# First layer's experts: the rows of two experts gathered in one indirect DMA onto 128 partitions and turned by eight transposes

## The reference, cut to what matters

```python
D_MODEL = 1024; N_EXPERTS = 32; EXPERT_HIDDEN = 512
...
    def expert_block(args):
        xe, e = args
        return (jax.nn.silu(xe @ w_gate[e]) * (xe @ w_up[e])) @ w_down[e]

    y = lax.map(expert_block, (xb, blk_e)).reshape(cap, d)
    out = jax.ops.segment_sum(y.astype(jnp.float32) * w_buf[:, None], tok_buf, num_segments=t + 1)
```

## Time and profile before

| what | value |
|---|---|
| median of the runs | 2399.06 us (2398.18, 2399.06, 2402.39) |
| span of the profiled execution | 2400.5 us |
| PE busy | 2173.3 us, 91% |
| DVE busy | 1108.4 us, 46% |
| ACT busy | 692.3 us, 29% |
| POOL busy | 215.8 us, 9% |
| data moved | 656.73 MB, 274 GB/s mean |
| first layer's experts | about 1198 to 1716 us of the span |
| second layer's experts | about 1907 to 2375 us |

### The profile page before, as it was taken

How to read it: one execution, slowest core, us unless ns; L and a number is a source line. 1 busy time by engine, 2 the same in 40 slices (tenths; PEclk the granted TensorE clock), 3 DMA queues, 4 the chain that set the end, 5 groups by cost and what they waited for, 6 DMA issues and landing times. The chain is left out here.

```text
span 2400.5 us, 29499 instructions
## 1 busy us (share of the span) xinstructions
PE 2173.3 (91%) x11404; PEld 1361.6 (57%) x11404; DVE 1108.4 (46%) x1760; ACT 692.3 (29%) x1102; POOL 215.8 (9%) x330
## 2 busy tenths in 40 slices
PE   7999999998899999988898888888788899999996
PEld 5778788876777888856633333333366533333332
DVE  5677655465676456577511111111587522222223
ACT  4243344344334443366111110110237111111110
POOL 2000000010000001100111111111120000000000
PEclk9989999999999999999799999998889899999998
DMA  8745576573655657501799999999830799999995
GB/s 295 260 151 190 193 235 202 184 277 135 226 206 193 211 171 248 163 2 39 301 335 401 411 409 411 406 408 411 302 84 8 299 380 428 428 428 429 428 428 230
DMA packets 175600, 656.73 MB, mean 274 GB/s; under 512 B 16295, under 2 KB 61943, under 8 KB 150288
## 3 DMA queue, kind: packets, MB, share of 16 engines
q1 hardware_dynamic: 159648, 622.65, 67.6%
q0 software_dynamic: 14032, 30.00, 4.0%
q10 hardware_dynamic: 1824, 2.73, 0.3%
HBM read 649.97 MB, written 23.79 MB: 281 GB/s over the span
## 5 line engine op out<-in xcount | busy, mean ns | idle before, releaser
L750 PE MATMUL bank<-sb_ring_rounded,sb_hT_rounded 128*128 128x512 f32 x2432 | 605.7, 397 | 18.7 <-DVE sb_ring_rounded L2045 8.4
L1382 PE MATMUL bank<-sb_ring,sb_arena 128*64 128x512 f32 x1984 | 491.1, 640 | 94.1 <-DMA sb_ring<-in_w_up 91.3
L750 PEld LDWEIGHTS bank<-sb_ring_rounded,sb_hT_rounded 128*128 128x128 f32 x2432 | 459.4, 191 | 119.5 <-issue 12.9
L1382 PEld LDWEIGHTS bank<-sb_ring,sb_arena 128*64 128x64 f32 x1984 | 152.4, 146 | 378.7 <-issue 372.9
L2045 DVE TENSOR_TENSOR sb_ring_rounded<-sb_ring,sb_ring_rounded 128x2048 fp32r<-128x2048 f32 (+1 forms) x142 | 314.9, 2258 | 112.4 <-ACT sb_ring_rounded L1516 107.4
L750 PE MATMUL bank<-sb_ring_rounded,sb_arena_rounded 128*128 128x512 f32 x1408 | 356.8, 395 | 7.6 <-DVE sb_arena_rounded L2032 7.0
L1516 ACT ACTIVATE sb_ring_rounded<-sb_ring 128x2048 fp32r<-128x2048 f32 x146 | 268.1, 1887 | 125.7 <-PE bank L750 100.1
L750 PEld LDWEIGHTS bank<-sb_ring_rounded,sb_arena_rounded 128*128 128x128 f32 x1408 | 266.1, 190 | 63.3 <-DVE sb_arena_rounded L2032 7.3
L1926 ACT ACTIVATE sb_hb<-bank 64x512 f32<-64x512 f32 x64 | 37.8, 590 | 697.4 <-PE bank L1382 697.4
L1406 PE MATMUL bank<-sb_ring,sb_arena 128*64 128x512 f32 x1008 | 233.4, 606 | 3.5 <-DVE sb_arena L2877 3.5
L2877 DVE COPY sb_arena<-bank 128x256 f32<-128x256 f32 x64 | 27.1, 424 | 319.2 <-PE bank L1393 319.1
(11 more groups left out here) (372 smaller groups left out, 2121.9 us busy)
## 6 DMA issues: line engine op xcount, KB each, us to landing
sb_ring<-in_w_down SPq DMA_DIRECT2D x63, 2048.0 KB, 22.0
sb_ring<-in_w_up SPq DMA_DIRECT2D x62, 2048.0 KB, 21.3
sb_ring<-in_w_gate SPq DMA_DIRECT2D x62, 2048.0 KB, 16.9
sb_ring<-in_w_ada SPq DMA_DIRECT2D x48, 1024.0 KB, 7.5
sb_ring<-in_ffn_w_gu SPq DMA_DIRECT2D x44, 1024.0 KB, 7.8
sb_ring<-in_xa_w_kv SPq DMA_DIRECT2D x16, 1024.0 KB, 7.3
sb_ring<-in_ffn_w_down SPq DMA_DIRECT2D x16, 1024.0 KB, 6.4
sb_ring<-in_od_w_in SPq DMA_DIRECT2D x12, 1024.0 KB, 7.7
```

Of the source, the lines that this page charges most:

```text
L750: ins = pe.matmul(bank[b][0:rows, :], rnd(x), rnd(w[:, k, :]), start=start and k == k0 and q == 0, stop=stop and k == k1 - 1 and q == len( ...
L1382: ins = pe.matmul(bank[2 * j + part][part * ROWS:(part + 1) * ROWS, :], mxT[:, j, k, :], w[:, k, :], start=k == 0, stop=k == KD - 1)
```

## The change

`mx` becomes one tile of 128 partitions: the rows of the even expert of a pair lie on partitions 0 to 63, those of the odd one on 64 to 127. The token part of `idx` gets a second half: partitions 64 to 127 hold the tokens of the next expert, so one column lists the rows of two experts. This takes a second DVE instruction of the same size, and POOL waits for both. There is one gather for a pair, at the head of POOL's pair (j = 0) and always through a copy into `pick`, the first one too. PE turns both experts at once by eight 128 x 128 transposes in the place behind the matmuls of the odd expert (j = 1), into two banks; ACT copies them out in two halves behind the odd expert's `silu`. ACT zeroes half as much. SP waits for the one gather where it waited for the first of two. The second layer is computed as before.

```diff
-        idx = spare[0:ROWS, :].bitcast(U32).rearrange("p (a b) -> p a b", a=2)
+        idx = spare[:, :].bitcast(U32).rearrange("p (a b) -> p a b", a=2)
...
-        mx = view(0, 2, D)
+        mx = view(0, D)
...
-                    sp.wait_ge(m["rows0"], 16)
+                    sp.wait_ge(m["rows"], 16)
...
-                def turn_rows(j, e, landed_rows):
-                    pe.wait_ge(m[f"rows{j}"], landed_rows * 16)
+                def turn_gathered(i):
+                    pe.wait_ge(m["rows"], (i + 1) * 16)
                     pe.sem_inc(s["passed"], 1)
                     for k in range(KD):
-                        ins = pe.transpose(bank[T0 + j][:, k * ROWS:(k + 1) * ROWS], mx[0:ROWS, j, k:D:KD], ident[0:ROWS, 0:ROWS])
-                    ins.then_inc(m["pe_xT"], 1)
+                        ins = pe.transpose(bank[T0 + k // 4][:, k % 4 * P:(k % 4 + 1) * P], mx[:, k:D:KD], ident)
+                        if k % 4 == 3:
+                            ins.then_inc(m["pe_xT"], 1)
...
-                        pe.wait_ge(m["xT"], i * 4 + 4 if l else e + 1)
+                        pe.wait_ge(m["xT"], i * 4 + 4 if l else i * 2 + 2)
...
-                        if l == 0 and not (last and j == 1):
-                            turn_rows(1 - j, e + 1, i + 1 + j)
+                        if l == 0 and j == 1 and not last:
+                            turn_gathered(i + 1)
...
-                    zeros = cst[:, C_WIN0:C_WIN0 + P].unsqueeze(1).to_broadcast([P, 2 * KD, P])
-                    act.activation(view(0, 2 * KD, P), zeros, ACT.Copy).then_inc(s["rows_zeroed"], 1)
+                    zeros = cst[:, C_WIN0:C_WIN0 + P].unsqueeze(1).to_broadcast([P, KD, P])
+                    act.activation(view(0, KD, P), zeros, ACT.Copy).then_inc(s["rows_zeroed"], 1)
...
-                        if l == 0 and more:
-                            turned_rows(1 - j, e + 1)
+                        if l == 0 and j == 1 and not last:
+                            placed_turned(i + 1)
...
-                dve.tensor_scalar(idx[:, 1, :], idx[:, 0, :], 1, None, ALU.logical_shift_right).then_inc(*c.up(s["idx_ready"]))
+                for half in range(2 - l):
+                    n = BLK * N_EXP - half
+                    dve.tensor_scalar(idx[half * ROWS:(half + 1) * ROWS, 1, 0:n], idx[0:ROWS, 0, half:half + n], 1, None, ALU.logical_shift_right).then_inc(*c.up(s["idx_ready"]))
...
-            def gather(j, e):
-                since(pool, m["pe_xT"], e - 1)
+            def gather(i):
+                since(pool, m["pe_xT"], i * 2)
                 apart()
-                if isinstance(e, int):
-                    pool.sem_inc(m["picked_in"], 1)
-                    at = column(1, e)
-                else:
-                    pool.tensor_copy(pick[:, 0, j:j + 1], column(1, e)).then_inc(m["picked_in"], 1)
-                    pool.wait_ge(m["picked_in"], e + 1)
-                    apart()
-                    at = pick[:, 0, j:j + 1]
-                pool.indirect_dma_start(out=mx[0:ROWS, j, :], out_offset=None, in_=DR["tok"],
-                                        in_offset=bass.IndirectOffsetOnAxis(ap=at, axis=0),
-                                        bounds_check=tiles * P - 1, oob_is_err=False).then_inc(m[f"rows{j}"], 16)
+                pool.tensor_copy(pick[:, 0, 0:1], column(1, i * 2, P)).then_inc(m["picked_in"], 1)
+                pool.wait_ge(m["picked_in"], i + 1)
+                apart()
+                pool.indirect_dma_start(out=mx, out_offset=None, in_=DR["tok"],
+                                        in_offset=bass.IndirectOffsetOnAxis(ap=pick[:, 0, 0:1], axis=0),
+                                        bounds_check=tiles * P - 1, oob_is_err=False).then_inc(m["rows"], 16)
...
-                    if l == 0 and not last:
-                        gather(j, i * 2 + j + 2)
+                    if l == 0 and j == 0 and not last:
+                        gather(i + 1)
...
-                gather(0, 0)
-                gather(1, 1)
+                gather(0)
```

More of the change, by code:

```diff
@@ L164, in build_program @@
         mod_g, mod_one = fix[0:96, 0, :], fix[0:96, 1, :]
-        pick = sb("pick", [ROWS, 2, 2], U32)
+        pick = sb("pick", [P, 2, 2], U32)
         steps_i = sb("steps_i", [P, 1], I32)
@@ L192, in loop_sems @@
         def loop_sems(l):
-            by_rows = ["places", "equals", "marked"] if l else ["rows0", "rows1", "picked_in"]
+            by_rows = ["places", "equals", "marked"] if l else ["rows", "picked_in"]
             names = ["landed%d" % q for q in range(SLOTS + 2 + l)] + by_rows + [
@@ L1445, in experts @@
                 if l == 0:
-                    turn_rows(0, 0, 1)
+                    turn_gathered(0)
                 expert_steps(pe, less_2, pair)
@@ L1889, in experts @@
                 m = moe[l]
-                def turned_rows(j, e):
-                    act.wait_ge(m["pe_xT"], e + 1)
-                    act.activation(mxT[:, j, :, :], bank[T0 + j][:, :].rearrange("p (k n) -> p k n", k=KD), ACT.Copy).then_inc(m["xT"], 1)
                 def rows_out(i):
@@ L1901, in placed_turned @@
                     for half in range(2):
-                        act.wait_ge(m["pe_xT"], i * 4 + half + 3)
+                        act.wait_ge(m["pe_xT"], i * 4 + half + 3 if l else i * 2 + half + 1)
                         act.activation(mxT[:, :, 4 * half:4 * half + 4, :], bank[T0 + half].rearrange("p (k j n) -> p j k n", k=4, j=2), ACT.Copy).then_inc(m["xT"], 1)
@@ L1921, in pair @@
                         e = i * 2 + j
-                        more = not (last and j == 1)
                         act.wait_ge(m["pe_hidden"], e + 1)
@@ L1953, in experts @@
                 if l == 0:
-                    turned_rows(0, 0)
+                    placed_turned(0)
                 expert_steps(act, less_2, pair)
@@ L3040, in experts, with column @@
                     pool.wait_ge(*c.next(s[f"tok_stored{q}"], 16 * tiles // 2))
-            pool.wait_ge(*c.next(s["idx_ready"]))
+            pool.wait_ge(*c.next(s["idx_ready"], 2 - l))
             def apart():
                 pool.sem_inc(s["passed"], 1)
-            def column(kind, e):
-                return idx[:, kind, e:e + 1] if isinstance(e, int) else idx[:, kind, bass.ds(e, 1)]
-            def gather(j, e):
-                since(pool, m["pe_xT"], e - 1)
+            def column(kind, e, rows=ROWS):
+                return idx[0:rows, kind, e:e + 1] if isinstance(e, int) else idx[0:rows, kind, bass.ds(e, 1)]
+            def gather(i):
+                since(pool, m["pe_xT"], i * 2)
                 apart()
-                if isinstance(e, int):
-                    pool.sem_inc(m["picked_in"], 1)
-                    at = column(1, e)
-                else:
-                    pool.tensor_copy(pick[:, 0, j:j + 1], column(1, e)).then_inc(m["picked_in"], 1)
-                    pool.wait_ge(m["picked_in"], e + 1)
-                    apart()
-                    at = pick[:, 0, j:j + 1]
-                pool.indirect_dma_start(out=mx[0:ROWS, j, :], out_offset=None, in_=DR["tok"],
-                                        in_offset=bass.IndirectOffsetOnAxis(ap=at, axis=0),
-                                        bounds_check=tiles * P - 1, oob_is_err=False).then_inc(m[f"rows{j}"], 16)
+                pool.tensor_copy(pick[:, 0, 0:1], column(1, i * 2, P)).then_inc(m["picked_in"], 1)
[4 more added lines that the diff above has]
+                                        bounds_check=tiles * P - 1, oob_is_err=False).then_inc(m["rows"], 16)
             def store(j, e):
-                pool.tensor_copy(pick[:, 1, j:j + 1], column(0, e)).then_inc(m["picked_out"], 1)
+                pool.tensor_copy(pick[0:ROWS, 1, j:j + 1], column(0, e)).then_inc(m["picked_out"], 1)
                 pool.wait_ge(m["picked_out"], e + 1)
@@ L3074, in store @@
                 apart()
-                pool.indirect_dma_start(out=DR["y"][l], out_offset=bass.IndirectOffsetOnAxis(ap=pick[:, 1, j:j + 1], axis=0),
+                pool.indirect_dma_start(out=DR["y"][l], out_offset=bass.IndirectOffsetOnAxis(ap=pick[0:ROWS, 1, j:j + 1], axis=0),
                                         in_=my[0:ROWS, j, :], in_offset=None,
```

2 lines of the change are left out of this document (1 added, 1 removed).

## The result

The changed kernel takes **2379.24 us** (median of 4 runs, 2377.72 to 2380.78); the kernel before, in the runs beside it, 2399.87 us (4 runs, 2398.18 to 2402.39). The ratio is 0.9913, 95% interval 0.9902 to 0.9925: 20.6 us less, where the forecast was no change (2399.6, range 2391.0 to 2404.5).

The account below looks back on a forecast made before the run. From 1280 us on the DMA weight stream was taken as the bound, so saved PE time becomes waiting. Terms +1.9 - 0.4 - 1.0 = +0.5 us on 2399.06 gave 2399.6 us, range 2391.0 to 2404.5.

Parts of the forecast that it names:

- Bytes of the gathers: Weight stream beside the first layer's gathers: bytes unchanged, loss of 21 us taken as unchanged, 0, between -21 and +21.
- The test named at the end: Forecast wrong if the middle's rate leaves 405 to 415 GB/s, gather windows change depth, or PE waits for rows or `xT`.
- The start: Second table instruction, copy, first 128-row gather and turning two experts before the first matmul: +1.9 us, between +0.3 and +4.2.
- Holes filled: Up to 1280 us, expert 1's matmuls follow at once and SP issues earlier, filling weight-stream holes: -0.4 us, at most -0.65.
- Later turnings: Eight transposes for sixteen in each later pair: PE gets about 1.0 us a pair, the up-weight wait grows, 0.
- POOL's order: Gather in POOL's queue behind the store at a pair's head lands after perhaps 13 us, needed 22 us later: 0.
- End of the stage: Last pair: expert 31's turning goes, PE is the bound and everything behind moves up, -1.0 us; 0 if something else holds.
- The faster one: Gathers spread over all partitions stop holding up the weights: half the loss gone 2389.1 us, all 2378.6; chance 0.13.
- The slower one: Twice the rows in flight hold up the weights more, 28 us instead of 21: +7, 2406.6 us; chance 0.08.
- The expensive start: Copy waits and 128 rows take POOL twice as long: +4.2 at the start, 2402.3 us or 2403.3; chance 0.09.

Follow-up runs that it names:

- the dropped rows: Both kernels with every token index out of bounds, gathers issued but all rows dropped: 2369.32 us for the kernel before, 2368.01 us for the changed one.
- narrow-transpose run: The changed kernel with sixteen 64-row transposes per pair, into one bank for each expert, instead of eight wide ones: 2383.13 us.
- the two 64-row gathers: The changed kernel with its 128-row gather issued as two of 64 rows, onto partitions 0 to 63 and 64 to 127: 2403.00 us.
- the padded one: The changed kernel with a second, nearly empty gather issued behind each gather: 2374.19 us, beside 2380.11 us for the changed kernel.
- the two with the 128-row form in the kernel before: The kernel before, 32 gathers issued over 128 partitions, half the rows dropped: 2390.92 us landing on partitions 0 to 63, 2380.39 us with halves in turn.
- doubled gathers: Each gather issued a second time: changed kernel, 128-row gathers onto an unread region, 2381.35 us; kernel before, 64-row gathers onto partitions 64 to 127, 2433.40 us.
- lower-half run: The kernel before with each gather issued over 128 partitions, upper half's indices out of bounds, rows still on partitions 0 to 63: 2390.92 us.

## Why the prediction was wrong

**The step that failed** is *Bytes of the gathers*: "I take the value of an unchanged number of rows, since few rows cost little and many cost much". The bound was right (21 us; the dropped rows price it at 20.9), the place was right (the gathers' windows), and the value inside the bounds was wrong: the same rows cost 20.9 us over their bytes in the 64-row form and 1.3 or less in the 128-row form. My reason for zero rested on two windows that differ in rows, and both were of 64 partitions, so they could say nothing on 128; between -21 and +21 the zero was a midpoint and not a reading. The test named at the end, a middle outside 405 to 415 GB/s, is what happened.

**The other steps.** *The start*, +1.9 forecast. From the end of the table's first instruction (1193.70, the middle of L2845's pair; 1197.15 before) to SP's load are 19.7 us for 17.74 before: +2.0. The sum was right and its terms were not, so this is luck. Table and copy cost 0.6 where 0.3 was forecast; from issue to the transposes there are 5.20 us for 5.85, so the 128 rows do not land 0.8 later but 0.65 earlier; turning costs 2.63 for 1.81, +0.8 as forecast; and expert 0's matmuls take 1.2 more up to SP's load (10.13 for 8.92), which the forecast did not have. The eight wide transposes need 1.95 us here, at a granted clock of 0.50, and not the 1.13 of the earlier trace rows, at 1.00: "the clock hardly matters" was wrong, and the +0.8 came out because the wait for ACT behind them is 0.69 us here for 1.44 there. The 1.2 us are the clock as well. These are the windows of 1209 to 1210 us, before and after, with the granted clock in the third column from the end:

```profile
1209.00:1210.00 1.00, 1.00 (x6) 0.28 (x4) 0.00 (x0) 0.00 (x0) 0.00 (x0) 0.69 0.88 377
```

```profile
1209.00:1210.00 1.00, 1.00 (x6) 0.31 (x4) 0.00 (x0) 0.00 (x0) 0.00 (x0) 0.82 0.30 107
```

By them the clock rose from 1.2 to 2.4 GHz at about 1209.6 and 1209.4 us, almost the same moment, but expert 0's matmuls had begun at 1205.97 and at 1203.28: 3.6 and 6.1 us of them ran at half speed, and half of the difference is 1.2 us.

*Holes filled*, -0.4, at most -0.65: too small. The first 65 us from SP's load on, in the kernel before and the changed one, then in both without rows:

```profile
1214.89:1279.89 65.00, 62.63 (x308) 24.75 (x308) 13.84 (x22) 10.08 (x17) 9.78 (x16) 1.00 0.99 379
```

```profile
1213.41:1278.41 65.00, 60.27 (x288) 22.53 (x286) 13.84 (x22) 9.75 (x17) 7.96 (x14) 0.99 0.99 404
```

```profile
1214.48:1279.48 65.00, 62.43 (x308) 24.66 (x309) 13.85 (x22) 10.09 (x17) 9.95 (x17) 1.00 0.97 384
```

```profile
1212.24:1277.24 65.00, 61.65 (x292) 22.98 (x290) 13.85 (x22) 9.75 (x17) 8.99 (x15) 0.98 0.98 401
```

Without rows the changed kernel still moves 401 GB/s for 384, which is worth 65 x 17/428 = 2.6 us of the stream, an estimate. No gather's form can do that; expert 1 follows without a gap (46 matmuls in one group), and SP issues the next weights sooner (7.6 us behind the first load, for 9.6). A share of 0.99 did not bound the holes at 0.65 us, since the share does not show the rate. In the middle, where the gathers' form acts, 375 x (426 - 409)/428 are 15 us of the stream, so that some 15 to 17 of the 19.6 us are the form's. Why the gain of the beginning does not show in the equal stretches of the two kernels without rows stays open; it is of the size of their scatter.

*Later turnings*, 0: right within the scatter, by the narrow-transpose run. But the wait for the up weights grew by 3.5 us and not 10 (69.9, 22 times, for 66.4, 25 times). That the weights, which came sooner too, took up the rest is argued and not shown.

*POOL's order*, 0: right. A gather lands after 11.7 us in the median and 14.2 at most (13 forecast), and PE waits for rows only once, at the start.

*End of the stage*, -1.0: nothing. The turning is gone from behind 1656.94, but the last up weights come at 1664.23, and PE waits 3.68 us for them: the time saved lies in a wait. "PE is the bound there" was true of the kernel before, where these matmuls begin at 1686.63 without a wait, and is not of the changed one.

**The rivals.** The faster one had the place and the size right, and as its mechanism the destination spread over all partitions, which the two 64-row gathers refute. The slower one expected deeper gather windows; they vanished. The expensive start came to half of its upper bound.

## What to carry to other kernels

Where a stream of weights over 128 partitions saturates the DMA engines, give every small load beside it the same 128-partition form, even if half of its rows are dropped, and then fill both halves evenly: here 1024 rows cost 30.7 us in the 64-row form and 11.0 or less in the other. Look for the loss in GB/s at a full share, not in the share: 410 and 426 GB/s both read 1.01. And where no row shows a resource in its new state, the middle of the bounds is not a forecast: give the ends their chances, and take a second trace of one kernel before reading differences of a few microseconds.

## What the runs showed that was not expected

The program's end is 6 us shorter in some kernels, whatever they compute. SP's last stores and the span, of the kernel before, the changed one and the padded one:

```profile
span 2400.5 us, 29499 instructions
...
2389.40 2.35 SPq L712 DMA_DIRECT2D out<-sb_hb  x2
```

```profile
2365.41 2.35 SPq L712 DMA_DIRECT2D out<-sb_hb  x2
```

```profile
span 2373.3 us, 29171 instructions
...
2368.20 2.35 SPq L712 DMA_DIRECT2D out<-sb_hb  x2
```

11.1 us from the store to the end of the span before and after, 5.1 in the padded kernel. The program's last instruction on POOL, which the views do not count as busy, lasts 10.5 to 10.7 us there in all kernels with up to 14,032 packets on the software queue, and 4.8 to 4.9 in the five with 16,080 or 16,592 (the two with the 128-row form in the kernel before, both with doubled gathers, the padded one). The padded run was made to test that and agreed (5.9 us between the medians); the changed kernel beside it has 10.7 us again. It is not the number of 128-row gathers, since the doubled 64-row gathers have none; whether it is the packets or something that goes with them stays open. It was what made the lower-half run look like half of the gain.

Also: the second load of the same 64 rows cost more over its bytes than the first (27.8 after 20.9 us), with PE's 5.4 us of waits for rows not taken apart from it. And of the lower-half run's missing 13.9 us the estimate leaves 4.1 open, about the scatter of the ruler; 3.1% of its weights' packets are still over 700 ns, and that an uneven load alone stretches packets was not shown.
